# Hybrid decoder trunk on one core: from the output projection to layer 1's projection, each stage's last part also prepares the next stage's first weights and tiles, and x is stored tile by tile

## The chip, the core and the metric

The kernel runs on one core of a Trainium2 chip. Its engines run side by side, each with its own queue of instructions: TensorE (PE, matrix products and transposes; PEld is its weight load), VectorE (DVE), ScalarE (ACT), GpSimd (POOL) and SyncE (SP), which issues the transfers (DMA) between the chip's memory and the on-chip buffers. They wait for each other only through semaphores. The metric is the time of one execution on the device in microseconds (us); lower is better.

## What is computed

Two decoder layers on x (1024 tokens x 1024 features, float32). Layer 0 mixes with two attentions of 8 heads each (one with a forget bias, one on 256 keys picked by an indexer), layer 1 with 16 heads of dilated attention. What follows the attention is the same in both layers, and it is what the change touches, with layer 1's first projection:

```python
x = x + merged @ w_out[i]                               # output projection
h = rmsnorm(x, norm_ffn[i])
x = x + conv_ffn(h, w_gate[i], w_up[i], conv_w[i], conv_b[i], w_down[i])
gate = jax.nn.sigmoid(rmsnorm(x, norm_ple[i]) @ w_ple_gate[i])
x = x + gate * (p[i] @ w_ple_proj[i])
...
def conv_ffn(h, w_gate, w_up, conv_w, conv_b, w_down):
    g = causal_dwconv(h @ w_gate, conv_w, conv_b)       # width 3, along the tokens
    return (jax.nn.gelu(g) * (h @ w_up)) @ w_down       # 2816 hidden features
```

`rmsnorm(x, g)` is x times the reciprocal root of its mean square over the features, times g.

## The kernel before

x stays on chip as 8 tiles of 128 tokens. The trunk (`trunk`) is a row of stages. From the attention of layer 0 on they are: output projection (`l0out`, function `output_stage`), feed-forward (`l0ff`, `ffn_stage`), per-layer gate (`l0pg`, `ple_stage`), layer 1's projection (`l1in`, `projection_stage`), layer 1's attention (`l1dil`), `l1out`, `l1ff`, `l1pg`, and a last stage, `load_stage`, that writes all of x with one transfer. Between two stages stands `recycle`: semaphores are cleared and all engines meet at a barrier, so that nothing of a stage begins before everything of the one ahead has ended. A stage's buffers are taken when it begins and given back when it ends.

**Products in three passes.** Every operand is split into a rounded part (hi) and the rest (lo), and `mm3` (L68 to L70) issues hi x lo, lo x hi and hi x hi: three matmuls of 128x128 by 512 columns. Weights arrive in a `raw` buffer with two places in chunks of 512 KB; ScalarE rounds a chunk to hi (128x1024) and GpSimd takes the rest, lo (128x1024; in the feed-forward's loop VectorE does that). The next chunk of a place is loaded once the lo of the old one is done.

**Feeding the tiles.** The class `Feed` turns x's tiles into the stationary or moving operands of a stage. For tile t: `square` (ScalarE, L129: sum of squares), `root` (GpSimd, L138 and L140: reciprocal root), `scale` (VectorE, L148: x times root times gain into one of two `xn` buffers), `turn` (TensorE, L160: 8 transposes of 128x128 into two banks of PSUM), `round` (ScalarE, L170: hi, twice 128x512) and `rest` (VectorE, L176: lo, twice 128x512). `ready` lets TensorE wait for the rest of a tile. In `output_stage` the tiles of `merged` need no norm, so there only turn, round and rest run.

**The stages.** `output_stage` and `projection_stage` walk over strips of 512 output columns (2 and 6), and in each over the 8 tiles; one unit (strip, tile) is 24 matmuls. Feed's first two tiles are turned before unit 0, and tile t + 2 after unit t of the first strip. The unit's sum is added to x (or copied) from one of four banks (`acc`). `ple_stage` has 16 units of 30 matmuls (24 for the gate, 6 for p's product), tiles 0 to 3 with strip 0, with strip 1, then tiles 4 to 7. `ffn_stage` runs 11 groups; a group is 4 units of 48 matmuls (two blocks of 128 hidden features, two halves of the tokens, gate and up), then 16 down products of 6 matmuls (m = 0 to 15, two for each tile), which use four banks in turn; VectorE adds each to x (L1952). Group 0 is written out and the other ten are a loop; ahead of group 0 tiles 0 to 3 are turned, tiles 4 to 7 in the middle of its first unit, and unit 1 waits until tile 7 is ready.

What sets the order is the program text of each engine; there is no planner. The last instructions of a stage are products and additions only, and the first ones of the next load the gain and the first weights, round them and feed the first tiles.

## Time and profile before

| | us |
|---|---|
| median of 3 runs (lowest to highest) | 3448.13 (3444.61 to 3450.27) |
| the profiled execution | 3450.76 |
| its span, first to last instruction | 3449.0 |
| TensorE busy | 3213.1 (93%) |
| VectorE / ScalarE / GpSimd busy | 1850.1 / 1269.2 / 729.8 |
| mean granted TensorE clock | 0.968 of full |

The profile has a page of totals, and the trace can be asked for waits, for the instructions of a stretch in order of time, for the busy time of stretches and for transfers. A row of the order in time gives the start, the length, the engine, the line, what is written from what, how many alike follow each other (x8), and in square brackets how long the engine had been idle before it and what it waited for. A start plus a length is an end. The length of a matmul overlaps the next, so the distance from start to start is its cost. Names carry the stage: `l0ff_d` is a tile of the feed-forward of layer 0, `k_x` is x.

### The profile page before, as it was taken

To read this page: it belongs to the slowest core of one execution; us is meant where nothing else is said; L and a number is where in the kernel's file an instruction comes from. 1 tells how busy PE (TensorE), PEld (TensorE's weight loads), DVE (VectorE), ACT (ScalarE), POOL (GpSimd) and SP (SyncE) were. 2 spreads that over 40 slices of the span, in tenths; PEclk is the share of its full clock that TensorE was granted. 3 is DMA by queue.
4 is the path that set the end of the run, shared out by engine and by line. 5 is a ranking of instruction groups with operands and counts; after the bars stand their busy time and mean duration, and the time that the engine had idled before them with its cause. 6 is when DMAs were issued, how large, how long until landed. Compare 5 with 4: busy or idle time off the path is not lost. (4 is left out here: it accounts for less than half of the span.)

```text
span 3449.0 us, 44902 instructions
## 1 busy us (share of the span) xinstructions
PE 3213.1 (93%) x15622; PEld 2673.8 (78%) x15622; DVE 1850.1 (54%) x3192; ACT 1269.2 (37%) x2716; POOL 729.8 (21%) x443
## 2 busy tenths in 40 slices
PE   7889997979979999999998998899879999999988
PEld 6657886968768888888776886799768888888866
DVE  4599997878234444444443331899324444443442
ACT  3274525868132222222132211788323222222231
POOL 3005444253220000000031541775220000000030
PEclk9999998989989999999999999899989999999999
DMA  4202233131221111111021323322112111111021
GB/s 138 73 21 92 92 116 81 37 69 37 97 68 61 55 42 49 45 52 36 5 74 52 95 97 122 70 67 54 49 31 86 49 44 53 49 37 61 0 79 49
DMA packets 268632, 214.55 MB, mean 62 GB/s; under 512 B 95164, under 2 KB 220908, under 8 KB 268524
## 3 DMA queue, kind: packets, MB, share of 16 engines
q1 hardware_dynamic: 268524, 213.17, 20.7%
q8 instruction: 60, 0.98, 0.1%
q14 instruction: 48, 0.39, 0.0%
HBM read 170.67 MB, written 41.94 MB: 62 GB/s over the span
## 5 line engine op out<-in xcount | busy, mean ns | idle before, releaser
L1961 DVE SCALAR_TENSOR_TENSOR l1ff_c<-l1ff_g,l1ff_cw,l1ff_c 128x512 f32<-128x512 f32 x44 | 33.1, 752 | 251.3 <-ACT l1ff_c L1870 251.3
L1961 DVE SCALAR_TENSOR_TENSOR l0ff_c<-l0ff_g,l0ff_cw,l0ff_c 128x512 f32<-128x512 f32 x44 | 33.1, 752 | 251.3 <-ACT l0ff_c L1870 251.3
L1750 DVE TENSOR_SCALAR_CACHE_REDUCE k_x<-k_x,l0in_cand 128x384 bf16<-128x384 f32 (+1 forms) x186 | 163.7, 942 | 1.1
L1952 DVE TENSOR_TENSOR k_x<-l0ff_d,k_x 128x512 f32<-128x512 f32 x176 | 119.4, 689 | 80.8 <-PE l0ff_d L70 80.8
L1952 DVE TENSOR_TENSOR k_x<-l1ff_d,k_x 128x512 f32<-128x512 f32 x176 | 119.4, 689 | 80.8 <-PE l1ff_d L70 80.8
L68 PE MATMUL l1in_acc<-l1in_w_lo,l1h_hi 128*128 128x512 f32 x384 | 151.1, 393 | 4.4 <-POOL l1in_w_lo L508 4.3
L69 PE MATMUL l1in_acc<-l1in_w_hi,l1h_lo 128*128 128x512 f32 x384 | 150.0, 391 | 0.0
L70 PE MATMUL l1in_acc<-l1in_w_hi,l1h_hi 128*128 128x512 f32 x384 | 149.9, 390 | 0.0
L132 POOL MEMSET l0pg_mhalf<- 128x8 f32 x1 | 0.1, 105 | 687.1 <-POOLq L107 687.1
L132 POOL MEMSET l1pg_mhalf<- 128x8 f32 x1 | 0.1, 104 | 687.1 <-POOLq L107 687.1
L68 PE MATMUL l1ff_gu<-l1ffn_lo,l1ff_w_hi_g 128*128 128x512 f32 x352 | 138.4, 393 | 7.4 <-DVE l1ff_cw L2000 5.5
L68 PE MATMUL l0ff_gu<-l0ffn_lo,l0ff_w_hi_g 128*128 128x512 f32 x352 | 137.8, 392 | 7.4 <-DVE l0ff_cw L2000 5.5
L70 PE MATMUL l1ff_gu<-l1ffn_hi,l1ff_w_hi_g 128*128 128x512 f32 x352 | 138.0, 392 | 0.0
L69 PE MATMUL l1ff_gu<-l1ffn_hi,l1ff_w_lo_g 128*128 128x512 f32 x352 | 138.0, 392 | 0.0
L70 PE MATMUL l0ff_gu<-l0ffn_hi,l0ff_w_hi_g 128*128 128x512 f32 x352 | 137.6, 391 | 0.0
L69 PE MATMUL l0ff_gu<-l0ffn_hi,l0ff_w_lo_g 128*128 128x512 f32 x352 | 137.5, 391 | 0.0
L68 PE MATMUL l0ff_gu<-l0ffn_lo,l0ff_w_hi_u 128*128 128x512 f32 x352 | 137.1, 390 | 0.0
L68 PE MATMUL l1ff_gu<-l1ffn_lo,l1ff_w_hi_u 128*128 128x512 f32 x352 | 137.1, 390 | 0.0
L70 PE MATMUL l1ff_gu<-l1ffn_hi,l1ff_w_hi_u 128*128 128x512 f32 x352 | 137.1, 389 | 0.0
L69 PE MATMUL l1ff_gu<-l1ffn_hi,l1ff_w_lo_u 128*128 128x512 f32 x352 | 137.1, 389 | 0.0
L70 PE MATMUL l0ff_gu<-l0ffn_hi,l0ff_w_hi_u 128*128 128x512 f32 x352 | 137.1, 389 | 0.0
L69 PE MATMUL l1ff_d<-l1ff_w_hi_d,l1ff_a_lo 128*128 128x512 f32 x352 | 137.1, 389 | 0.0
(465 smaller groups left out, 9720.6 us busy)
## 6 DMA issues: line engine op xcount, KB each, us to landing
l0w_raw<-in_w_in_even SPq DMA_DIRECT2D x24, 512.0 KB, 4.1
l1in_raw<-in_w_in_odd SPq DMA_DIRECT2D x24, 512.0 KB, 3.8
l0ff_raw_g<-in_w_gate SPq DMA_DIRECT2D x22, 512.0 KB, 4.0
l0ff_raw_u<-in_w_up SPq DMA_DIRECT2D x22, 512.0 KB, 5.3
l0ff_raw_d<-in_w_down SPq DMA_DIRECT2D x22, 512.0 KB, 4.9
l1ff_raw_g<-in_w_gate SPq DMA_DIRECT2D x22, 512.0 KB, 4.0
l1ff_raw_u<-in_w_up SPq DMA_DIRECT2D x22, 512.0 KB, 5.2
l1ff_raw_d<-in_w_down SPq DMA_DIRECT2D x22, 512.0 KB, 4.9
```

The costliest lines, as they stand in the source:

```text
L68: pe.matmul(out, a_hi, b_lo, start=start, stop=False)
L69: pe.matmul(out, a_lo, b_hi, start=False, stop=False)
L70: return pe.matmul(out, a_hi, b_hi, start=False, stop=stop)
L132: pool.memset(self.half[:], -0.5).then_inc(self.mean, 1)
L1750: tick(dve.tensor_scalar(hits[:, cols], score[:, cols], cand[:, i:i + 1].bitcast(F32), 0.0, ALU.is_ge, ALU.add, accum_out=cnt[:, i:i + 1]))
L1952: dve.tensor_tensor(cols, ps_d[:, m % 4, :], cols, ALU.add).then_inc(added, 1)
L1961: dve.scalar_tensor_tensor(c[:, half, :], g[:, at - 1:at + 511], cw[:, 1, bass.ds(blk, 1)], c[:, half, :], ALU.mult, ALU.add).then_inc(con ...
```

## The change

**Two feeds in a stage.** Where a stage has a successor, its last part runs the successor's steps besides its own, with a second feed (`nfeed`) and a second set of semaphores (`n_...`):

- `output_stage`: once all of merged is turned, SP loads the norm gain and the feed-forward's first two blocks of gate and up weights; when strip 0 is done (8 units) ScalarE rounds them (4 pieces of 128x1024), GpSimd takes the 4 rests and only then the roots; tiles 0 to 6 of x are squared, scaled, turned, rounded and rested during strip 1, tile t being turned after unit t + 1 of the strip. Tile 7 (`LAST`) is left to the feed-forward, which turns it in the middle of its first unit, with the convolution's weights.
- `ffn_stage`: the last of the 11 groups is written out for TensorE too. SP loads the gate stage's gain, its first five weight chunks and half of p once the last group's weights are split; ScalarE rounds the chunks after its last unit, with squares of tiles 0 to 4 between them; GpSimd alternates rests and roots; VectorE scales and rests tiles 0 and 1 between the additions of the last down products; TensorE turns them after tile 4 and tile 5 of the down products.
- `ple_stage` of layer 0: four squares and two tiles of `l1in` are fed during units 8 to 11, its first strip of weights is split during units 12 to 15.
- The stages that follow begin with that done: a few `sem_inc` stand for it, and their feeds begin at tile `first` (2, or 7 in the feed-forward), their roots at `first_root`.

**Fixed places.** So that a stage's operands outlive its barrier, the buffers of these stages lie at fixed addresses (`sb(..., at=)`): hi and lo of the tiles, the strips, and a region for the rest, shared one after the other. Two tiles of `l1in` go to slots that the gate stage no longer reads (`slot`).

**The store.** `load_stage` and the barrier ahead of it are gone; in layer 1's gate stage SP writes tile t of x (512 KB) once its last addition is done.

The shapes of the loads, roundings, transposes and matmuls, and what each stage multiplies, stay as they are. Of the stages ahead of `l0out` and of `l1dil` nothing moves. The diff, cut to the moved steps:

```diff
...
+MERGED_AT, HI_AT, LO_AT, STRIP_AT = (32 * n * KB for n in range(4))
+EXTRA_AT, SMALL_AT = 160 * KB, 172 * KB
...
     def scale(self, dve, t):
+        n = t - self.first
         if t == 0:
             dve.wait_ge(self.gain_in, 16)
-        if t >= 2:
-            dve.wait_ge(self.turned, 2 * (t - 1))
-        dve.wait_ge(self.rooted, t + 1)
-        dve.scalar_tensor_tensor(self.xn[:, t % 2, :], self.src[:, t, :], self.rstd[:, t:t + 1], self.g[:],
+        if n >= 2:
+            dve.wait_ge(self.turned, 2 * (n - 1))
+        if t >= self.first_root:
+            dve.wait_ge(self.rooted, t - self.first_root + 1)
...
+        feed = Feed(st, x, hi, lo, [[tp[:, 2 * i + h, :] for h in range(2)] for i in range(2)], ident, buf.gain, buf.norm,
+                    slot=buf.slot, first=AHEAD, first_root=ROOTS)
...
+            for b in range(2):
+                sp.sem_inc(raw_in[b], 16 * CH // 2)
...
+            act.sem_inc(hi_ready, CH)
...
-            feed.scale(dve, 0)
-            feed.scale(dve, 1)
-            feed.rest(dve, 0)
-            feed.scale(dve, 2)
-            feed.rest(dve, 1)
+            feed.scale(dve, AHEAD)
...
-            feed.turn(pe, 0)
-            feed.turn(pe, 1)
...
+            sp.wait_ge(feed.turned, 2 * NT)
+            nfeed.load(sp)
+            for b in range(2):
+                for dst, src in zip(nxt.raw, nxt.sources):
+                    sp.dma_start(dst[:, b, :].rearrange("p (k n) -> p k n", n=P),
+                                 src[:, b * P:(b + 1) * P].rearrange("(k p) n -> p k n", p=P)).then_inc(n_raw_in[b], 16)
...
+            act.wait_ge(filled, NT)
+            split_next(0)
+            split_next(1)
+            for t in range(AHEAD):
+                act.wait_ge(added, NT + t + 1)
+                nfeed.square(act, t)
+                if t:
+                    nfeed.round(act, t - 1)
+            nfeed.round(act, AHEAD - 1)
...
+            nfeed.prepare(pool)
+            for k in range(4):
+                n, b = k % 2, k // 2
+                pool.wait_ge(n_hi_ready, k + 1)
+                pool.tensor_tensor(nxt.w_lo[n][:, b, :], nxt.raw[n][:, b, :], nxt.w_hi[n][:, b, :].bitcast(F32),
+                                   ALU.subtract).then_inc(n_lo_ready, 1)
+            for t in range(AHEAD):
+                nfeed.root(pool, t)
...
+                if s == 1 and t:
+                    nfeed.rest(dve, t - 1)
+                if s == 1 and t < AHEAD:
+                    nfeed.scale(dve, t)
...
+                if s == 1 and t:
+                    nfeed.turn(pe, t - 1)
...
+            if nxt is not None:
+                sp.wait_ge(lo_ready, CH)
+                nxt.load(sp, 0, n_raw_in[0])
+                nxt.load(sp, 1, n_raw_in[1])
+                sp.wait_ge(feed.scaled, NT - AHEAD)
+                nfeed.load(sp)
+                for n in range(2, nxt.CH):
+                    sp.wait_ge(n_lo_ready, n - 1)
+                    nxt.load(sp, n, n_raw_in[n % 2])
+            else:
+                for t in range(NT):
+                    sp.wait_ge(added, t + 5 if t < 4 else t + 9)
+                    sp.dma_start(final[t * P:(t + 1) * P, :], x[:, t, :]).then_inc(stored, 16)
+                sp.wait_ge(stored, 16 * NT)
...
+                if i < CH - 2:
+                    split(2 + i)
+                if nxt is not None and i >= 12:
+                    n = i - 12
+                    act.wait_ge(n_raw_in[n % 2], 16 * (n // 2 + 1))
+                    act.activation(nxt.chunk(0, n)[0], nxt.raw[:, n % 2, :, :], ACT.Copy).then_inc(n_hi_ready, 1)
+                if nxt is not None and 8 <= i < 8 + nxt.ROOTS:
+                    act.wait_ge(added, i - 3)
+                    nfeed.square(act, i - 8)
+                if nxt is not None and 10 <= i < 10 + nxt.AHEAD:
+                    nfeed.round(act, i - 10)
...
+                if nxt is not None and i == 9:
+                    dve.wait_ge(feed.turned, 2 * (NT - AHEAD))
+                if nxt is not None and 9 <= i < 9 + nxt.AHEAD:
+                    nfeed.scale(dve, i - 9)
+                if nxt is not None and 10 <= i < 10 + nxt.AHEAD:
+                    nfeed.rest(dve, i - 10)
...
-            feed.turn(pe, 0)
...
-            feed.turn(pe, 1)
...
+                if nxt is not None and 9 <= i < 9 + nxt.AHEAD:
+                    feed.ready(pe, i - 3)
+                    nfeed.turn(pe, i - 9)
...
+            for n in range(2):
+                for b in range(2):
+                    sp.sem_inc(raw_in[n][b], 16)
...
+            sp.wait_ge(w_lo_done, 6 * NG)
+            nfeed.load(sp)
+            for n in range(nxt.CH):
+                if n >= 2:
+                    sp.wait_ge(n_lo_ready, n - 1)
+                nxt.load(sp, n, n_raw_in[n % 2])
+            nxt.load_p(sp, 0, n_p_in)
+            sp.wait_ge(n_p_in, 16)
...
+            act.sem_inc(w_hi_done, 4)
+            feed.square(act, LAST)
+            feed.round(act, LAST)
...
+            def square_next(t):
+                act.wait_ge(added, 16 * NG - 10 + 2 * t)
+                nfeed.square(act, t)
+
+            for n in range(nxt.CH):
+                if n == nxt.CH - 1:
+                    act.wait_ge(lo_done, 4 * NG)
+                act.wait_ge(n_raw_in[n % 2], 16 * (n // 2 + 1))
+                act.activation(nxt.chunk(0, n)[0], nxt.raw[:, n % 2, :, :], ACT.Copy).then_inc(n_hi_ready, 1)
+                if n >= 2:
+                    square_next(n - 2)
+            nfeed.round(act, 0)
+            square_next(3)
+            nfeed.round(act, 1)
+            square_next(4)
...
+            pool.sem_inc(w_lo_done, 4)
...
+            nfeed.prepare(pool)
+            for n in range(nxt.CH):
+                pool.wait_ge(n_hi_ready, n + 1)
+                n_hi, n_lo = nxt.chunk(0, n)
+                pool.tensor_tensor(n_lo, nxt.raw[:, n % 2, :, :], n_hi.bitcast(F32), ALU.subtract).then_inc(n_lo_ready, 1)
+                if n >= 2:
+                    nfeed.root(pool, n - 2)
+            for t in range(nxt.CH - 2, nxt.ROOTS):
+                nfeed.root(pool, t)
...
+                    if last and m % 2 == 1 and m >= 7:
+                        t = (m - 7) // 2
+                        if t < nxt.AHEAD:
+                            nfeed.scale(dve, t)
+                        if 1 <= t < 1 + nxt.AHEAD:
+                            nfeed.rest(dve, t - 1)
...
+                        if feeding and b == 0 and half == 1:
+                            feed.ready(pe, LAST)
...
+                            if feeding and b == 0 and half == 0 and n == 0:
+                                pe.wait_ge(cw_in, 32)
+                                pe.transpose(ps_gu[:, 1, 1, 0:4 * NFB], cw4[:], ident[0:4 * NFB, 0:4 * NFB]).then_inc(cw_t, 1)
+                                feed.turn(pe, LAST)
...
+                    if last and 4 <= t < 4 + nxt.AHEAD:
+                        nfeed.turn(pe, t - 4)
...
-            with pe.Fori(0, NG - 1) as i:
...
+            with pe.Fori(0, NG - 2) as i:
...
+            body(NG - 1, True)
...
-        load_stage(nc, "store", [(tiles(out[0]), x[:])])
...
```

VectorE, from the last additions of `l0out` (`l0out_acc`) into the feed-forward; `l0ff_raw_d` serves as the feed-forward's `xn`, `l0ffn_lo` and `k_lo` are the tiles' rests. Before:

```order
L652 TENSOR_TENSOR k_x<-l0out_acc,k_x 128x512 x11
L87 UNCONDITIONAL_BRANCH
L1939 UNCONDITIONAL_BRANCH
L1989 MEMSET l0ff_g 128x2
L148 SCALAR_TENSOR_TENSOR l0ff_raw_d<-k_x,l0ff_rstd,l0ff_gain 128x1024 x2
L176 TENSOR_TENSOR l0ffn_lo<-l0ff_d,l0ffn_hi 128x4x128 x2
```

The same place now:

```order
L757 TENSOR_TENSOR k_x<-l0out_acc,k_x 128x512 x4
L164 SCALAR_TENSOR_TENSOR l0ff_raw_d<-k_x,l0ff_rstd,l0ff_gain 128x1024
L757 TENSOR_TENSOR k_x<-l0out_acc,k_x 128x512
L193 TENSOR_TENSOR k_lo<-l0out_tp,k_hi 128x4x128 x2
L164 SCALAR_TENSOR_TENSOR l0ff_raw_d<-k_x,l0ff_rstd,l0ff_gain 128x1024
```

The first scale stands between the additions of units 8 and 9, and from then on each addition is followed by the rests of one tile and the scale of the next; the branches (the stage's end) come seven tiles later.

VectorE at the end of `l0ff`, in the last group's down products. Before:

```order
L1973 TENSOR_TENSOR l0ff_a_lo<-l0ff_act_f,l0ff_a_hi 128x512
L1952 TENSOR_TENSOR k_x<-l0ff_d,k_x 128x512 x14
L87 UNCONDITIONAL_BRANCH
L793 UNCONDITIONAL_BRANCH
L148 SCALAR_TENSOR_TENSOR l0pg_xn<-k_x,l0pg_rstd,l0pg_gain 128x1024 x2
```

The same place now:

```order
L2094 TENSOR_TENSOR l0ff_a_lo<-l0ff_act_f,l0ff_a_hi 128x512
L2073 TENSOR_TENSOR k_x<-l0ff_d,k_x 128x512 x6
L164 SCALAR_TENSOR_TENSOR l0pg_xn<-k_x,l0pg_rstd,l0pg_gain 128x1024
L2073 TENSOR_TENSOR k_x<-l0ff_d,k_x 128x512 x2
L164 SCALAR_TENSOR_TENSOR l0pg_xn<-k_x,l0pg_rstd,l0pg_gain 128x1024
L193 TENSOR_TENSOR k_lo<-l0ff_gu,k_hi 128x4x128 x2
L2073 TENSOR_TENSOR k_x<-l0ff_d,k_x 128x512 x2
L193 TENSOR_TENSOR k_lo<-l0ff_gu,k_hi 128x4x128 x2
L2073 TENSOR_TENSOR k_x<-l0ff_d,k_x 128x512 x4
```

The first scale now stands ahead of the additions m = 8 to 15, the second scale and the rests of two tiles ahead of the later ones.

## Rows read from the trace of the kernel before

**Rows 1.** The page, part 1: busy us, share of the span, instructions.

```profile
PE 3213.1 (93%) x15622; PEld 2673.8 (78%) x15622; DVE 1850.1 (54%) x3192; ACT 1269.2 (37%) x2716; POOL 729.8 (21%) x443
```

**Rows 2.** Order in time, l0out to l0ff: start, length, engine, line, tiles, [idle].

```profile
968.63 0.69 DVE L652 TENSOR_TENSOR k_x<-l0out_acc,k_x 128x512 f32<-128x512 f32 x1 [4.75 <-PE l0out_acc L70]
970.14 0.33 SPq L124 DMA_DIRECT2D l0ff_gain<-in_norm_ffn  x1
975.79 3.67 PE L160 MATMUL l0ff_d<-k_square,l0ff_raw_d 128*128 128x128 f32 x16 [7.21 <-DVE l0ff_raw_d L148]
1012.59 0.47 PE L68 MATMUL l0ff_gu<-l0ffn_lo,l0ff_w_hi_g 128*128 128x512 f32 x1 [1.94 <-issue]
```

**Rows 3.** Order in time, l1out to l1ff: TensorE's first row and unit 1.

```profile
2550.06 3.67 PE L160 MATMUL l1ff_d<-k_square,l1ff_raw_d 128*128 128x128 f32 x16 [7.26 <-DVE l1ff_raw_d L148]
2588.16 0.47 PE L68 MATMUL l1ff_gu<-l1ffn_lo,l1ff_w_hi_g 128*128 128x512 f32 x1 [1.94 <-issue]
```

**Rows 4.** Order in time, l0out: units with turns, then an addition without.

```profile
894.07 1.04 PE L160 MATMUL l0out_tp<-k_square,l0m_merged 128*128 128x128 f32 x8
900.44 1.03 PE L160 MATMUL l0out_tp<-k_square,l0m_merged 128*128 128x128 f32 x8
925.18 0.69 DVE L652 TENSOR_TENSOR k_x<-l0out_acc,k_x 128x512 f32<-128x512 f32 x1 [4.75 <-PE l0out_acc L70]
```

**Rows 5.** Order in time: one step each of square, root, scale, lo and hi.

```profile
972.52 1.06 ACT L129 ACTIVATE l0ff_g<-k_x 128x1024 f32<-128x1024 f32 x1
974.03 0.55 POOL L140 TENSOR_TENSOR l0ff_rstd<-l0ff_ss,l0ff_mhalf 128x1 f32<-128x1 f32 x1
979.03 1.28 DVE L148 SCALAR_TENSOR_TENSOR l0ff_raw_d<-k_x,l0ff_rstd,l0ff_gain 128x1024 f32<-128x1024 f32 x1
896.83 2.40 POOL L638 TENSOR_TENSOR l0out_w_lo<-l0out_raw,l0out_w_hi 128x1024 fp32r<-128x1024 f32 x1 [18.25 <-ACT l0out_w_hi L621]
1727.54 1.06 ACT L733 ACTIVATE l0pg_w_hi<-l0pg_raw 128x1024 fp32r<-128x1024 f32 x1 [3.53 <-DMA l0pg_raw<-in_w_ple_gate]
```

**Rows 6.** Order in time, last group of l0ff to l0pg's unit 1.

```profile
1698.11 0.39 PE L68 MATMUL l0ff_d<-l0ff_w_lo_d,l0ff_a_hi 128*128 128x512 f32 x1
1702.66 0.63 ACT L1877 ACTIVATE l0ff_a_hi<-l0ff_act_f 128x512 fp32r<-128x512 f32 x1 [0.84 <-DVE l0ff_act_f L1969]
1720.07 0.69 DVE L1952 TENSOR_TENSOR k_x<-l0ff_d,k_x 128x512 f32<-128x512 f32 x1 [0.67 <-PE l0ff_d L70]
1748.93 0.48 PE L68 MATMUL l0pg_ps_g<-l0pg_w_lo,l0pg_hi 128*128 128x512 f32 x1
```

**Rows 7.** Order in time, the same of layer 1: last addition, turn ahead of unit 1.

```profile
3295.68 0.69 DVE L1952 TENSOR_TENSOR k_x<-l1ff_d,k_x 128x512 f32<-128x512 f32 x1 [0.67 <-PE l1ff_d L70]
3325.24 1.10 PE L160 MATMUL l1pg_tp<-k_square,l1pg_xn 128*128 128x128 f32 x8
```

**Rows 8.** Order in time, l0pg to l1in: last addition, first turn of the dense part.

```profile
1858.08 0.69 DVE L821 TENSOR_TENSOR k_x<-k_x,l0pg_sg 128x512 f32<-128x512 f32 x1
1880.52 1.04 PE L160 MATMUL l1in_tp<-k_square,l1in_xn 128*128 128x128 f32 x8
```

**Rows 9.** Last addition; transfers: count, KB each, median us to landing.

```profile
3435.34 0.69 DVE L821 TENSOR_TENSOR k_x<-k_x,l1pg_sg 128x512 f32<-128x512 f32 x1
...
vsplit<-l1in_vout SPq DMA_DIRECT2D x16, 512.0 KB, 2.6
...
l0pg_raw<-in_w_ple_gate SPq DMA_DIRECT2D x8, 512.0 KB, 3.8
```

**Rows 10.** Stretch, length, busy PE PEld DVE ACT POOL, granted clock, DMA share, GB/s.

```profile
864.00:868.00 4.00, 0.04 (x1) 0.00 (x0) 1.23 (x2) 2.60 (x3) 2.31 (x2) 0.93 0.58 219
867.00:871.00 4.00, 2.82 (x7) 2.27 (x8) 0.00 (x0) 0.00 (x0) 3.37 (x2) 0.60 0.41 119
1873.00:1877.00 4.00, 0.84 (x4) 0.67 (x4) 1.88 (x3) 3.25 (x5) 2.74 (x2) 1.00 0.33 115
```

More of the change, by code:

```diff
@@ L203, in index_projection_stage @@
         tp = st.ps("tp", [P, 4, 512])
-        feed = Feed(st, x, hi, lo, [[tp[:, 2 * i + h, :] for h in range(2)] for i in range(2)], ident, gain, junk=feat[:])
+        norm = Norm(st, st.sb("xn", [P, 2, D]), feat[:], st.sb("gain", [P, D]))
+        feed = Feed(st, x, hi, lo, [[tp[:, 2 * i + h, :] for h in range(2)] for i in range(2)], ident, gain, norm)
         square_in, tail_in, angle_in = st.sem("square_in"), st.sem("tail_in"), st.sem("angle_in")
@@ L403, in _, with __init__, slot, chunk @@
                         mm.then_inc(tok_done, 1)
-def projection_stage(nc, name, x, gain, hi, lo, ident, strips, proj, vsplit, stats):
-    S = len(strips)
+class HeadsBuffers:
+    CH = 4
+    AHEAD = 2
+    ROOTS = 4
+    def __init__(self, st, hi, lo, gain, strips):
+        self.hi, self.lo, self.gain, self.strips = hi, lo, gain, strips
+        self.raw = st.sb("raw", [P, 2, KD // self.CH, 512], at=MERGED_AT)
+        self.w_hi = [st.sb(f"w_hi{b}", [P, KD, 512], F32R, at=STRIP_AT + 32 * b * KB) for b in range(2)]
+        self.w_lo = [st.sb(f"w_lo{b}", [P, KD, 512], F32R, at=STRIP_AT + (32 * b + 16) * KB) for b in range(2)]
+        self.norm = Norm(st, st.sb("xn", [P, 2, D], at=MERGED_AT + 8 * KB), st.sb("junk", [P, D], at=MERGED_AT + 16 * KB)[:],
+                         st.sb("gain", [P, D], at=MERGED_AT + 24 * KB), SMALL_AT + 256)
+    def slot(self, t):
+        return (t + self.AHEAD) % NT
+    def chunk(self, s, c):
+        rows = (slice(None), slice(c * KD // self.CH, (c + 1) * KD // self.CH))
+        return self.w_hi[s % 2][rows], self.w_lo[s % 2][rows]
+    def load(self, sp, n, arrived):
+        s, c = n // self.CH, n % self.CH
+        size = D // self.CH
+        sp.dma_start(self.raw[:, n % 2, :, :], self.strips[s][c * size:(c + 1) * size, :]
+                     .rearrange("(k p) n -> p k n", p=P)).then_inc(arrived, 16)
@@ L421, in projection_stage @@
         acc = st.ps("acc", [P, 4, 512])
         tp = st.ps("tp", [P, 4, 512])
-        feed = Feed(st, x, hi, lo, [[tp[:, 2 * i + h, :] for h in range(2)] for i in range(2)], ident, gain)
+        feed = Feed(st, x, hi, lo, [[tp[:, 2 * i + h, :] for h in range(2)] for i in range(2)], ident, buf.gain, buf.norm,
+                    slot=buf.slot, first=AHEAD, first_root=ROOTS)
         raw_in = [st.sem(f"raw_in{b}") for b in range(2)]
@@ L517, in _ @@
             pool.memset(half[:], -0.5).then_inc(rstd_step, 1)
+            pool.sem_inc(lo_ready, CH)
             feed.prepare(pool)
-            feed.root(pool, 0)
-            feed.root(pool, 1)
-            low(0)
-            low(1)
-            feed.root(pool, 2)
-            low(2)
-            low(3)
-            for t in range(3, NT):
+            for t in range(ROOTS, NT):
                 feed.root(pool, t)
@@ L718, in _ @@
-            feed.load(sp)
-            load(0)
-            load(1)
-            load_p(0)
-            for n in range(2, 2 * CH):
-                load(n)
-                if n == CH:
-                    sp.wait_ge(p_turned, 2)
-                    load_p(1)
+            for n in range(CH, 2 * CH):
+                if n >= CH + 2:
+                    sp.wait_ge(lo_ready, n - CH - 1)
+                buf.load(sp, n, raw_in[n % 2])
+            sp.wait_ge(p_turned, 2)
+            buf.load_p(sp, 1, p_arrived)
@@ L742, in _ @@
-            feed.square(act, 1)
-            split(0)
-            feed.round(act, 0)
-            split(1)
-            feed.square(act, 2)
             p_round(0)
             p_round(1)
-            split(2)
-            feed.round(act, 1)
-            split(3)
-            split(4)
-            for t in range(3, NT):
+            for t in range(ROOTS, NT):
                 feed.square(act, t)
+            split(0)
+            split(1)
             for i, (s, t) in enumerate(UNITS):
@@ L807, in _ @@
             p_rest(1)
-            feed.rest(dve, 1)
             feed.scale(dve, 3)
```

446 lines of the change are left out of this document (206 added, 240 removed).

## The prediction

> **What bounds the kernel now.** I read the page's totals first: TensorE is busy 3213.1 of 3449.0 us [rows 1], so only its idle time can be won without taking work away. Then I asked for its instructions in order of time around each end of a stage; the reader is to see there how long it idles and what it waits for. The places are alike. The last product of l0out ends at 975.79 - 7.21 = 968.58, the last addition at 969.32; SyncE issues the next stage's first load at 970.14, so the barrier costs 0.8 us. Then everything hangs on the gain's load, the scales and the first weights, and TensorE is dense and undisturbed only from unit 1 on, at 1012.59 [rows 2]. There are five such ends: two out to feed-forward, two feed-forward to gate, one gate to layer 1's projection; a sixth is the store. Inside the stages TensorE is the bound: without turns an addition waits 4.75 us and takes 0.69, a pitch of 5.44 for 24 matmuls (0.227 each); with a turn it is 900.44 - 894.07 = 6.37 [rows 4]. So a turn moved into dense work costs 0.92 us, and 30 matmuls cost 6.80.
>
> I cost each end as an interval: from the last product of a stage to a point in the next from which both kernels do the same.
>
> **Out to feed-forward.** Before: 1012.59 - 968.58 = 44.0 us in layer 0 [rows 2], 2588.16 - (2550.06 - 7.26) = 45.4 in layer 1 [rows 3]. Now, counted from the same product:
> - Seven turns during strip 1: 7 x 0.92 = 6.4.
> - A wait ahead of the first of them. The four roundings start when strip 0 is done, about 925.2 [rows 4]; GpSimd needs four rests, each 2.40 [rows 5], from 926.3 to 936.0, and only then takes the first root (0.55 and a small step before it, 0.8), so VectorE's scale (1.28) ends at 938.2, while TensorE wants tile 0 at 936.0: 2.3 us. VectorE's addition behind it slips too, but four banks cover it. From the second tile on the loop addition, square (1.06 and the read of its sum, 1.25), root 0.8, scale 1.28, with two rests of 0.69 between, takes about 5.3 of the 6.37 us between two turns: 1 us of slack, no further wait.
> - The tail: after the last turn, round and rest, which the row at 1012.59 prices at 1.94 (there too TensorE waits for the last tile's rest), and the barrier 0.8: 2.8.
> - The feed-forward's unit 0, 48 matmuls = 10.9 with one turn and the small transpose of the convolution's weights, 1.0. The tile's square, root and scale (3.4) end before the first half (5.4); the convolution's two small loads now stand first in SyncE's queue.
>
> Sum 6.4 + 2.3 + 2.8 + 11.9 = 23.4. **Gain 20.6 and 22.0.** The loads (2.6 MB from about 914 on, when SyncE has nothing left) have 11 us until ScalarE wants them; they lie beside products.
>
> **Feed-forward to gate.** Let D be the start of the last group's down products, 1698.11; before, the last addition ends at 1720.76 = D + 22.7, and unit 1 of the gate stage starts at 1748.93 = D + 50.8 [rows 6]. In layer 1 the last addition ends at 3296.37, and unit 1 follows the turn at 3325.24 by 0.9: 29.7 us later against 28.2 [rows 7]. Now the chain of the first tile decides. ScalarE's last unit ends at 1703.3 = D + 5.2 [rows 6]; then chunk 0 is rounded (1.06 [rows 5]) to D + 6.3, its rest (2.4) to 8.9, chunk 2's load, which waits for that place, to 12.7 (3.8 to landing [rows 9]), rounding 13.8, rest 16.2, and only then root(0) 17.0, scale 18.4. TensorE has come to the first turn at D + 13.6 (10 products of 1.36): it waits 4.8 us. The rest follows from the same durations: load 4 to D + 20.1, its rounding and a square to 22.4, round(0) 23.5, rest(0) 24.3, the additions m = 10 and 11, rest(1) 26.8, last product 28.4, last addition D + 29.4, that is 6.7 later than before. In the gate stage: barrier 0.8, p's eight transposes 0.9, unit 0 6.8, a turn 0.9: unit 1 at D + 38.8 against D + 50.8. **Gain 12.0 and 13.6.** Here the edit gives a new wait, and queued behind the waiting scale are the additions m = 8 to 15, for which TensorE's four banks wait.
>
> **Gate to layer 1's projection.** Two turns during units 9 and 10 cost 1.8. The squares, the two scales and the weight chunks (one per unit of 6.8; load, rounding, rest together 7.3, in two places) lie beside products. The last addition ends at 1858.77; the next stage's unit 0 begins after 0.8 at 1859.6 + 1.8 = 1861.4, and ends at 1866.8, where it meets the turn that stood at 1880.52 [rows 8]. **Gain 13.7.**
>
> **Store.** Before, 3449.0 - 3436.0 = 13.0 us stand after the last addition [rows 9]. Now only the last tile's 512 KB are outstanding: the other direction (chip memory to buffer) of that size takes 3.8 to landing, the kernel's own writes of that size 2.6 [rows 9]; I take the writes, being the same kind, and 0.6 around them: 3.3. Bounds 3.2 to 5. **Gain 9.7.**
>
> **The clock.** After TensorE has idled, its granted clock may fall from 2.4 to 1.2 GHz. In the stretch 864 to 868 it was busy 0.04 us, and in 867 to 871 the clock was 0.60; yet in 1873 to 1877, with 3.2 us idle, it stayed at 1.00 [rows 10]. The new version has seven waits of 2.3 to 4.8 us: two at the first turn, two of 2.8 and one of about 3 at barriers, two of 4.8. A stretch like 867 to 871 (0.4 of 4 us lost) costs 1.6; I let three of the seven meet it: 5 us lost, bounds 0 and 11. The Trainium skill (TensorE: Matmul & The Clock Gate, Part 1) says that a gap drops the clock to half, that when it happens depends on where the gap falls, and advises against idle gaps between bursts of matmuls: that speaks against the new waits. [...]
>
> **Sum.** 20.6 + 22.0 + 12.0 + 13.6 + 13.7 + 9.7 = 91.6, less 5 = 86.6. The profiled execution took 3450.76, 1.8 above its span and 2.6 above the median; 3448.1 - 86.6 = 3361.5, so **3362 us**. What isn't in the sum: everything ahead of l0out, l1in's later strips and l1dil have the same instructions in the same order, cost 0. ScalarE's order has as many table loads as before (8), so squares between gelu and sigmoid add none. TensorE's last group written out instead of looped: no price in the trace, but straight text runs at the loop's pitch; taken as 0, bounds 0 to 3 for two.
>
> **Rivals.**
> - *The chain of the tiles is slower than its slack.* In strip 1 square, root, rest and scale have 1 us of slack per tile, and GpSimd and VectorE share the work. If every turn waited 1.5 us more, 2 x 7 x 1.5 = 21, and if the last group's waits grew by 2 us each, 4: 3387. For it: five steps over three engines, each passed on by a semaphore. Against it: every duration has a row, and the handovers are small beside them. Chance 0.17, at 3372 to 3390.
> - *The waits I reckon are not there.* If GpSimd's rests are quicker beside an idle VectorE or the chunk loads land sooner, 4 x 2 us come back, and no clock falls: 5 more: 3349. Chance 0.13, at 3345 to 3354.
> - *The next stage doesn't start at once.* The preparation is done, but the first product still waits, for its stage's code or for a semaphore. Then each of five ends would keep some 7 us of the idle time: 3397. The row at 970.14 shows an engine active 0.8 us after the last addition, which speaks against it. Chance 0.04.
> - *Slower than before: the fixed places.* All operands of TensorE move to new addresses. If a matmul there cost more, the two feed-forwards alone have 6336 of them (44 units x 48 and 176 x 6, twice): from 0.014 us each, 6% of 0.227, on, the gain of 87 is eaten. With 10% it would be 3362 + 144 = 3506. Against it: the pitch of 0.227 is that of l0out and of the down products (1.36 for 6) alike, whose buffers lie apart. Chance 0.02.
>
> **How the numbers follow.** The forecast, 3354 to 3372, has 0.64; its size hangs on the clock (0 to 11) and the two waits. Two in ten may lie outside: the range takes in all of the forecast, nearly all of the second rival and the nearer part of the first, 3349 to 3384. A measurement of this kernel tells 0.2% (7 us) from no change; only the last rival is on the other side. Faster 0.97, within 0.2% 0.01, slower 0.02.
>
> **What would show it.** Right: TensorE's wait ahead of the first turn in strip 1 is 2 to 3 us and absent ahead of the other six; the idle time between l0out and l0ff is 3 us instead of 26 with turns; in the last group TensorE waits some 5 us for a scale behind `root`, and the stage ends 6 to 7 us later after D; l1in's first product comes 3 us after the last of l0pg; 3 to 4 us between the last addition and the end. Wrong: a wait at each turn (first rival), a first product that waits for "issue" (third), a pitch above 5.44 for a unit (fourth), or a clock at half in more than three of the seven places.

## The result, and the profile after

The changed kernel takes 3372.4 us (median of 4 runs, 3370.4 to 3373.2) against 3448.8 for the kernel before (again 4 runs); the ratio is 0.978, 95% interval 0.976 to 0.980. It is faster by 76 us, 10 less than the forecast of 86.6: inside the range of 3349 to 3384, and 0.4 above the upper end of the forecast's own 3354 to 3372. Measured again later in another series it took 3372.2 (3368.1 to 3375.8).

The page of the changed kernel, totals, to be held against [rows 1]:

```profile
PE 3198.6 (95%) x15622; PEld 2663.5 (79%) x15622; DVE 1850.8 (55%) x3192; ACT 1268.2 (38%) x2716; POOL 729.2 (22%) x448
```

The work is the same; the span is 3371.1, so TensorE's idle time fell from 235.9 to 172.5 us. The remaining 14.5 of the 77.9 us of span are busy time: fewer matmuls run at half clock (the mean granted clock is 0.977 where it was 0.968).

**Out to feed-forward.** The changed kernel in order of time; these rows answer to [rows 2, 3]:

```profile
932.94 1.96 PE L177 MATMUL l0out_tp<-k_square,l0ff_raw_d 128*128 128x128 f32 x8 [2.22 <-DVE l0ff_raw_d L164]
940.98 1.04 PE L177 MATMUL l0out_tp<-k_square,l0ff_raw_d 128*128 128x128 f32 x8
...
976.85 0.47 PE L73 MATMUL l0ff_gu<-k_lo,l0ff_w_hi_g 128*128 128x512 f32 x1 [3.06 <-PEq L2168]
984.07 1.04 PE L177 MATMUL l0ff_d<-k_square,l0ff_raw_d 128*128 128x128 f32 x8
...
2515.44 0.47 PE L73 MATMUL l1ff_gu<-k_lo,l1ff_w_hi_g 128*128 128x512 f32 x1 [3.08 <-PEq L2168]
```

The first turn waits 2.22 us, the other six not at all, and the feed-forward's first product comes 3.06 us behind the last one of the stage ahead (3.08 in layer 1). So the stalls are where they were reckoned. What is longer is busy time: from the first turn to the second 8.04 us instead of 6.37, from the first product of the feed-forward to the turn of tile 7 7.22 instead of 5.44.

**Feed-forward to gate.** The last group, VectorE, GpSimd and TensorE together (the last row is p's transposes, the gate stage's first work on TensorE); they answer to [rows 6]:

```profile
1675.86 0.39 PE L73 MATMUL l0ff_d<-l0ff_w_lo_d,l0ff_a_hi 128*128 128x512 f32 x1
...
1692.68 2.34 POOL L2054 TENSOR_TENSOR l0pg_x_lo<-l0pg_raw,l0pg_x_hi 128x1024 fp32r<-128x1024 f32 x1
1692.81 3.28 DVE L164 SCALAR_TENSOR_TENSOR l0pg_xn<-k_x,l0pg_rstd,l0pg_gain 128x1024 f32<-128x1024 f32 x1 [5.18 <-POOL l0pg_rstd L154]
...
1696.15 1.97 PE L177 MATMUL l0ff_gu<-k_square,l0pg_xn 128*128 128x128 f32 x8 [6.53 <-DVE l0pg_xn L164]
1696.74 2.37 POOL L2054 TENSOR_TENSOR l0pg_p_lo<-l0pg_raw,l0pg_p_hi 128x1024 fp32r<-128x1024 f32 x1
1697.22 2.98 DVE L164 SCALAR_TENSOR_TENSOR l0pg_xn<-k_x,l0pg_rstd,l0pg_gain 128x1024 f32<-128x1024 f32 x1
...
3235.14 1.97 PE L177 MATMUL l1ff_gu<-k_square,l1pg_xn 128*128 128x128 f32 x8 [6.92 <-DVE l1pg_xn L164]
...
3249.54 1.06 PE L934 MATMUL l1pg_ps_p<-k_square,l1pg_ptile 128*128 128x128 f32 x8 [1.73 <-PEq L115]
```

The scale is an instruction of 1.28 us [rows 5]. Here it takes 3.28 and 2.98, both times beside a rest that GpSimd began just before it. TensorE waits 6.53 us in layer 0 and 6.92 in layer 1 where 4.8 was reckoned; unit 1 of the gate stage starts at D + 43.0 in layer 0 and D + 43.6 in layer 1, not at 38.8.

**Gate to projection, and the end.** Rows that answer to [rows 8, 9]:

```profile
1831.82 0.47 PE L73 MATMUL l1in_acc<-k_w_lo,k_hi 128*128 128x512 f32 x1 [3.02 <-PEq L115]
1837.39 1.04 PE L177 MATMUL l1in_tp<-k_square,k_xn 128*128 128x128 f32 x8
...
3367.34 0.69 DVE L923 TENSOR_TENSOR k_x<-k_x,l1pg_sg 128x512 f32<-128x512 f32 x1
3368.06 0.33 SPq L832 DMA_DIRECT2D out<-k_x  x1
```

The first product of layer 1 comes 3.02 us after the last of the gate stage; 3.0 us stand between the last addition and the end, where 13.0 stood before.

**The clock.** The 6 us that follow each of the seven idle stretches of the changed kernel (columns as in [rows 10]; the granted clock is the third number from the end):

```profile
932.94:938.94 6.00, 6.00 (x24) 5.16 (x25) 3.03 (x4) 2.12 (x4) 0.75 (x2) 0.72 0.01 3
976.85:982.85 6.00, 6.00 (x19) 4.79 (x20) 1.28 (x1) 0.59 (x2) 0.74 (x2) 0.72 0.03 8
1696.15:1702.15 6.00, 6.00 (x21) 5.07 (x22) 5.84 (x6) 3.59 (x7) 5.22 (x6) 0.60 0.01 3
1831.82:1837.82 6.00, 6.00 (x28) 4.97 (x29) 1.28 (x1) 0.23 (x1) 0.18 (x2) 1.00 0.31 90
2473.19:2479.19 6.00, 6.00 (x31) 5.12 (x32) 3.03 (x4) 2.12 (x4) 0.76 (x2) 1.00 0.01 3
2515.44:2521.44 6.00, 6.00 (x19) 4.78 (x20) 1.28 (x1) 0.60 (x2) 0.74 (x2) 0.72 0.03 9
3235.14:3241.14 6.00, 6.00 (x20) 5.10 (x21) 6.00 (x6) 3.81 (x7) 5.26 (x6) 0.56 0.06 22
```

TensorE's clock has two levels, 1.2 and 2.4 GHz, so 0.72 over 6 us means that part of them ran at 1.2 GHz; 0.28 x 6 = 1.7 us of work are lost. That is the 1.67 and nearly all of the 1.8 by which the stretches above are longer. The clock fell behind five of the seven: 0.28, 0.28, 0.40, 0.28 and 0.44 of 6 us, 10.1 us in all.

### The profile page after: what moved, and what is told of

Same layout as the page of the kernel before. It is cut to its first block and busy times, and to the rows that moved or that the text cites. A ratio compares the mean times of both kernels' runs of the same rounds, so it can differ in the third digit from the quotient of the medians.

```text
span 3371.1 us, 44871 instructions
## 1 busy us (share of the span) xinstructions
PE 3198.6 (95%) x15622; PEld 2663.5 (79%) x15622; DVE 1850.8 (55%) x3192; ACT 1268.2 (38%) x2716; POOL 729.2 (22%) x448
## 5 line engine op out<-in xcount | busy, mean ns | idle before, releaser
L73 PE MATMUL l1in_acc<-k_w_lo,k_hi 128*128 128x512 f32 x384 | 150.2, 391 | 3.1 <-PEq L115 3.0
L75 PE MATMUL l1in_acc<-k_w_hi,k_hi 128*128 128x512 f32 x384 | 149.5, 389 | 0.0
L74 PE MATMUL l1in_acc<-k_w_hi,k_lo 128*128 128x512 f32 x384 | 149.4, 389 | 0.0
L73 PE MATMUL l1ff_gu<-k_lo,l1ff_w_hi_g 128*128 128x512 f32 x352 | 137.7, 391 | 3.1 <-PEq L2168 3.1
L73 PE MATMUL l0ff_gu<-k_lo,l0ff_w_hi_g 128*128 128x512 f32 x352 | 137.7, 391 | 3.1 <-PEq L2168 3.1
L73 PE MATMUL l1ff_d<-l1ff_w_lo_d,l1ff_a_hi 128*128 128x512 f32 x352 | 137.9, 392 | 0.0
L73 PE MATMUL l0ff_d<-l0ff_w_lo_d,l0ff_a_hi 128*128 128x512 f32 x352 | 137.9, 392 | 0.0
L75 PE MATMUL l0ff_gu<-k_hi,l0ff_w_hi_g 128*128 128x512 f32 x352 | 137.6, 391 | 0.0
L75 PE MATMUL l1ff_gu<-k_hi,l1ff_w_hi_g 128*128 128x512 f32 x352 | 137.6, 391 | 0.0
L74 PE MATMUL l1ff_gu<-k_hi,l1ff_w_lo_g 128*128 128x512 f32 x352 | 137.5, 391 | 0.0
```

The costliest lines, as they stand in the source:

```text
L73: pe.matmul(out, a_hi, b_lo, start=start, stop=False)
L74: pe.matmul(out, a_lo, b_hi, start=False, stop=False)
L75: return pe.matmul(out, a_hi, b_hi, start=False, stop=stop)
```

## The experiments

All start from the changed kernel. Theory A says what cost the ff-to-gate ends their gain: a scale that meets GpSimd's rest stands until the rest is done. Theory C says what cost the out-to-ff ends theirs: half clock behind idle stretches.

### E1: the rests wait for the scale

```diff
             for n in range(nxt.CH):
                 pool.wait_ge(n_hi_ready, n + 1)
+                if n >= 3:
+                    pool.wait_ge(nfeed.scaled, n - 2)
                 n_hi, n_lo = nxt.chunk(0, n)
```

> The changed kernel; in the last feed-forward group GpSimd takes the rests of weight chunks 3 and 4 only once VectorE's scale of tile 0, or tile 1, is done. Theory A (a scale, which reads two operands from the on-chip buffer, stands still while GpSimd takes a rest): both scales (L164) of l0ff and l1ff fall from 3.28 and 2.98 us to about 1.28, TensorE's wait ahead of the first turn from 6.5 to 4.6, and the stage ends some 2 us sooner after the start of the down products, though GpSimd's rests are 1.4 us later. Rival B (the scales are long for another reason, such as ScalarE's work or TensorE's transposes at the half clock): they stay near 3 us, the wait stays 6.5, and the stage ends no sooner, or 1 us later.

Layer 0's last group in this kernel, VectorE, GpSimd, TensorE:

```profile
1696.30 1.28 DVE L164 SCALAR_TENSOR_TENSOR l0pg_xn<-k_x,l0pg_rstd,l0pg_gain 128x1024 f32<-128x1024 f32 x1 [5.37 <-POOL l0pg_rstd L154]
1697.64 1.97 PE L177 MATMUL l0ff_gu<-k_square,l0pg_xn 128*128 128x128 f32 x8 [4.72 <-DVE l0pg_xn L164]
1697.72 2.35 POOL L2056 TENSOR_TENSOR l0pg_x_lo<-l0pg_raw,l0pg_x_hi 128x1024 fp32r<-128x1024 f32 x1 [1.53 <-DVE l0pg_xn L164]
```

All four scales are back at 1.28 or 1.29 us, and TensorE waits 4.72 and 4.65, as the prediction had reckoned with 1.28. Unit 1 of the gate stage starts at D + 40.5 in both layers, 2.5 and 3.1 earlier than in the changed kernel. Of that the shorter wait is 1.8 and 2.3; the rest, 0.7 to 0.8, is clock, which in the 6 us behind the wait is 0.74 and 0.72 here and was 0.60 and 0.56. The 1.7 that remain to 38.8 are what 0.74 and 0.72 still cost. The single run, 3370.3, is 2 us below the changed kernel, which one run can't tell from its scatter; the verdict rests on the rows. (The rows gain 5.6 us; but in this execution the clock also fell behind layer 1's first turn in the output stage and ahead of layer 1's projection, 1.7 us each, where the changed kernel's kept it.)

### E2a and E2b: the same collision made, and avoided, in the output stage

There the changed kernel takes all four rests, then the roots, and no scale meets a rest. E2a takes root 0 behind the second rest, so that the third meets the scale; E2b also holds the third rest until the scale is done (the line with the wait; E2a lacks it).

```diff
             for k in range(4):
                 n, b = k % 2, k // 2
+                if k == 2:
+                    nfeed.root(pool, 0)
+                    pool.wait_ge(nfeed.scaled, 1)
                 pool.wait_ge(n_hi_ready, k + 1)
...
-            for t in range(AHEAD):
+            for t in range(1, AHEAD):
                 nfeed.root(pool, t)
```

> The changed kernel; in the output stage GpSimd takes the root of tile 0 after two of the four weight rests instead of after all four, and the third rest follows at once, beside VectorE's scale of tile 0. If the 2.2 us wait ahead of the first turn came from the root's place alone, it is gone (the root is ready 3 us sooner, and the scale takes 1.28). Theory A (a scale stands still beside a rest) says that the first scale now takes 2.4 + 1.3 = about 3.5 us, and that some 1 us of the wait stays in both layers.

> As the run before, but the third weight rest waits until tile 0's scale is done. Theory A: the scale takes 1.28 us, no wait ahead of the first turn (2.2 us before), output stages 2.2 us shorter each, and 1 to 2 us more where the wait had let TensorE's clock fall. Rival B: the same as the run before, whatever its scale took.

E2a in layer 0, then E2b in the same place:

```profile
930.53 2.39 POOL L742 TENSOR_TENSOR l0ff_w_lo_g<-l0ff_raw_g,l0ff_w_hi_g 128x1024 fp32r<-128x1024 f32 x1
930.68 3.31 DVE L164 SCALAR_TENSOR_TENSOR l0ff_raw_d<-k_x,l0ff_rstd,l0ff_gain 128x1024 f32<-128x1024 f32 x1 [2.23 <-POOL l0ff_rstd L154]
934.05 1.09 PE L177 MATMUL l0out_tp<-k_square,l0ff_raw_d 128*128 128x128 f32 x8 [0.89 <-DVE l0ff_raw_d L164]
```

```profile
930.88 1.28 DVE L164 SCALAR_TENSOR_TENSOR l0ff_raw_d<-k_x,l0ff_rstd,l0ff_gain 128x1024 f32<-128x1024 f32 x1 [2.23 <-POOL l0ff_rstd L154]
932.24 2.40 POOL L743 TENSOR_TENSOR l0ff_w_lo_g<-l0ff_raw_g,l0ff_w_hi_g 128x1024 fp32r<-128x1024 f32 x1 [1.48 <-DVE l0ff_raw_d L164]
933.20 1.03 PE L177 MATMUL l0out_tp<-k_square,l0ff_raw_d 128*128 128x128 f32 x8
```

The collision can be made at will: 3.31 us where the changed kernel has 1.28, and gone again with the one wait. The idle stretch of 2.2 at the first turn was GpSimd's order, rests first: 0.89 with the collision, none without, in both layers. One run each, 3365.6 and 3364.5, so 7 and 8 us below the changed kernel and too close to tell them apart; what tells them apart is the rows.

### E3: squares ahead of the third chunk, each root behind its rest

```diff
-            for n in range(nxt.CH):
+            def split_next(n):
...
-                if n >= 2:
-                    square_next(n - 2)
+            split_next(0)
+            split_next(1)
+            for t in range(3):
+                square_next(t)
+            split_next(2)
             nfeed.round(act, 0)
+            split_next(3)
             square_next(3)
             nfeed.round(act, 1)
+            split_next(4)
             square_next(4)
...
-                if n >= 2:
-                    nfeed.root(pool, n - 2)
-            for t in range(nxt.CH - 2, nxt.ROOTS):
-                nfeed.root(pool, t)
+                nfeed.root(pool, n)
```

> The changed kernel; in the last feed-forward group ScalarE squares tiles 0 to 2 before it rounds chunk 2, and GpSimd takes root n right after the rest of chunk n (not of chunk n + 2). By the chain of the prediction with theory A: root(0) is ready near D + 9.3 (D: start of the last down products), so no wait ahead of the first turn, and the last addition falls at about D + 24.3 instead of D + 33.3: 9 us less for each of two layers, 18 in all, near 3354. Rival: the end of the stage hangs on the last weight chunk's load, rounding and rest and not on the tiles; then it ends at D + 28 or later and the gain is under 10 us in all.

3356.5 us (3356.0 to 3357.4; ratio to the kernel before 0.973, 0.971 to 0.975), 16 below the changed kernel. In layer 0:

```profile
1691.01 1.37 DVE L164 SCALAR_TENSOR_TENSOR l0pg_xn<-k_x,l0pg_rstd,l0pg_gain 128x1024 f32<-128x1024 f32 x1
1692.93 1.03 PE L177 MATMUL l0ff_gu<-k_square,l0pg_xn 128*128 128x128 f32 x8
1693.73 2.81 DVE L164 SCALAR_TENSOR_TENSOR l0pg_xn<-k_x,l0pg_rstd,l0pg_gain 128x1024 f32<-128x1024 f32 x1
1696.60 1.09 PE L177 MATMUL l0ff_gu<-k_square,l0pg_xn 128*128 128x128 f32 x8
```

No turn waits. The first tile was late because its root stood behind the third chunk, whose load waits for a place in `raw`; the tile itself was done long before. Unit 1 is at D + 34.2 and D + 34.3, so 8.8 and 9.3 earlier than in the changed kernel: 18.1 in the rows, 16 in the medians. The second scale still meets a rest (2.81), and here that costs nothing, since TensorE has two down products (2.7 us) to do meanwhile.

### E4: TensorE busy up to the barrier

Six matmuls more behind the last turn of the output stage, into a bank that nobody reads:

```diff
                 if s == 1 and t:
                     nfeed.turn(pe, t - 1)
+            pe.wait_ge(added, NT * S - 1)
+            for k in range(6):
+                pe.matmul(acc[:, 0, :], hi[:, k, 7 * P:8 * P], w_hi[1][:, k, :], start=k == 0, stop=k == 5)
```

> Starts from the changed kernel. After the last prepared turn of the output stage TensorE runs six matmuls more, whose result nobody reads (a hi tile and weights that lie there), so that it stands idle only across the barrier. Theory C (about 1.7 us of the shortfall of each output stage's end is TensorE at half clock in the first matmuls of the feedforward, after the two idle stretches of 2.2 and 3.1 us in front of them): the stretch idle ahead of the feedforward falls from 3.07 to about 1.8, its first half unit takes 5.4 instead of 7.2 us in both layers, and the span is 3 to 4 us shorter (3367.5). Rival D (the clock falls because of the stretch of 2.2 us before the first turn, or with the place in the program whatever stands before it): the first half unit stays at 7.2 and the span within 1 us of the changed kernel's 3371.

Layer 0:

```profile
974.73 1.63 PE L785 MATMUL l0out_acc<-l0out_w_hi,k_hi 128*128 128x512 f32 x6
978.07 0.47 PE L73 MATMUL l0ff_gu<-k_lo,l0ff_w_hi_g 128*128 128x512 f32 x1 [1.71 <-PEq L2171]
983.71 1.04 PE L177 MATMUL l0ff_d<-k_square,l0ff_raw_d 128*128 128x128 f32 x8
```

The idle stretch is 1.71 us (1.69 in layer 1), and the first half unit takes 5.64 and 5.63 us instead of 7.22 and 7.23, as theory C expects. By itself this trace doesn't show it, since C9 below has the same 5.63 without the six matmuls. Over the eleven traces of kernels with the change the clock fell behind 14 of the 18 stretches of 3.1 us at this place, and behind none of the four of 1.7 (here and in E8); that supports theory C. Rival D is out: the stretch of 2.2 us at the first turn is still there in this kernel, and in E2a, E2b and E7, where it is gone, the clock fell at this place behind five of six. The median, 3369.1 (3366.3 to 3370.5), is 3.3 lower; the expected 3 to 4 are no more than what two runs of one kernel differ by, as C9 shows.

### C9: the changed kernel once more

> The changed kernel as it is, in the same series as the kernel above, so that the two are compared on one chip: 3372 us, its scales beside GpSimd's rests again near 3.1 us each in the feedforward's last group, and waits of 2.2 and 6.7 us at the first turns. Rival (these were chance of one execution): scales at 1.28 and waits of 4.8.

```profile
979.93 0.47 PE L73 MATMUL l0ff_gu<-k_lo,l0ff_w_hi_g 128*128 128x512 f32 x1 [3.06 <-PEq L2168]
985.56 1.04 PE L177 MATMUL l0ff_d<-k_square,l0ff_raw_d 128*128 128x128 f32 x8
...
1694.77 3.29 DVE L164 SCALAR_TENSOR_TENSOR l0pg_xn<-k_x,l0pg_rstd,l0pg_gain 128x1024 f32<-128x1024 f32 x1 [5.64 <-POOL l0pg_rstd L154]
```

The scales are long again (3.29 and 3.17, 3.28 and 2.98), the waits 2.22, 2.21, 6.99 and 6.84: theory A is no accident of one execution. But the half unit behind 3.06 us of idle time takes 5.63 here: the same kernel with the same idle stretch kept its clock this time, and this execution, the fastest of its five, has a span of 3366.4, 4.7 shorter. So what an idle stretch costs in clock differs from execution to execution, and E4's gain by its median can't be told from that.

### E5: the store as before

```diff
-            else:
+            elif final is not None:
...
-                ple_stage(nc, L + "pg", x, ple, ident, final=out[0])
+                ple_stage(nc, L + "pg", x, ple, ident)
+                recycle(nc)
+        with Stage(nc, "store") as st:
...
+                sp.dma_start(out[0].rearrange("(t p) c -> p t c", p=P), x[:]).then_inc(moved, 16)
+                sp.wait_ge(moved, 16)
```

> Undoes the store alone: in layer 1's gate stage the last additions write x again and the whole of x goes out behind the stage in one transfer of 4 MB, as in the kernel before. The theory (the store by tiles gives 9.7 to 9.9 us, all of it at the end): 3382 us, the time from the last addition to the end of the span back at 15.1 from 5.1 us. Rival (part of that gain was lost again ahead of the end, because fifteen transfers that leave during the stage slow its weights or the additions): under 9, the stage's last products earlier than in the changed kernel by the difference.

```profile
3366.03 0.69 DVE L923 TENSOR_TENSOR k_x<-k_x,l1pg_sg 128x512 f32<-128x512 f32 x1
3367.54 0.38 SPq L2259 DMA_DIRECT2D out<-k_x  x1
```

3384.1 us (3381.4 to 3385.8), 11.7 above the changed kernel. From the last addition to the end of the span (3379.6) it is 12.9 against 3.0: 9.9 for the store. (The 15.1 and 5.1 of the expectation count from the last product; measured 15.0 and 5.1.) Ahead of the end there is no sign of a price: from unit 1 of layer 1's gate stage to its last product it is 107.7 us here and 107.5 in the changed kernel, with the transfers beside it. The medians differ by 1.8 more than the rows, which is within the scatter of the runs.

### E6: no tiles ahead for layer 1's projection

`HeadsBuffers` with `AHEAD = 0` and `ROOTS = 0`: the weights are still prepared in the gate stage, the two tiles are squared, scaled, split and turned in the projection's own.

> Undoes one part of the last boundary alone: layer 0's gate stage still prepares the weights of layer 1's projection, but not its first two tiles; these are squared, scaled, split and turned in the projection's own stage. The theory (at this boundary the turned tiles are worth more than the weights, whose halves come early in the stage anyhow): the first product unit of layer 1's projection starts about 8.7 us later behind the last product than in the changed kernel, less the 1.8 us that the two turns no longer take in the gate stage: 3379.3 us. Rival (the weights carry the gain, and the tiles' chain hides behind their arrival): within 2 us of 3372.

```profile
1837.27 3.78 PE L177 MATMUL l1in_tp<-k_square,k_xn 128*128 128x128 f32 x16 [6.67 <-DVE k_xn L164]
...
1846.36 1.03 PE L177 MATMUL l1in_tp<-k_square,k_xn 128*128 128x128 f32 x8
```

3376.7 us (3373.4 to 3379.7), 4.4 above the changed kernel; 6.9 was expected and at most 2 by the rival. From the end of l0pg's last product to the turn of tile 2 it was 1880.52 - 1856.7 = 23.8 us before, is 1846.36 - 1830.6 = 15.8 here and 1837.39 - 1828.8 = 8.6 in the changed kernel. So the weights alone bring 8.0 to 8.1, the tiles 7.2 less the 1.8 of their two turns, 5.3 to 5.4, together the 13.4 of this end. That the tiles are worth more than the weights was wrong.

### E7: both repairs; E8: with the six matmuls too

E7 is E3 and E2b in one, E8 adds E4's edit.

> Both repairs together, on the changed kernel: at the feedforward's end ScalarE squares tiles 0 to 2 before it copies chunk 2, and GpSimd takes each root right behind the rest of the same number; at the output stage's end GpSimd takes the first root before its third weight rest, and holds that rest until the first scale is done. The theory has the two gains add, since they lie at different ends: 16 us from the first, 6 to 8 from the second (two ends, 2.2 us of wait and up to 1.8 us of clock each): 3349 us, no wait at any first turn. Rival (the second's gain is no more than the two waits of 2.2 us, since the clock falls at the barrier anyhow): 3352. A second rival: the clock's mean falls as the stage ends close up, and it stays at 3355.

> The two repairs together with the six matmuls that keep TensorE busy to the output stage's barrier. In the kernel with the two repairs the first half unit of the feedforward took 7.24 us in layer 0 and 7.21 in layer 1, behind idle stretches of 3.06 and 3.11. Theory C, that this is TensorE at half clock and costs 1.6 us at each end: both fall to 5.6, the idle stretches to 1.7, and the time to 3345. Rival: the half clock then comes at another stretch idle (the boundary of 3.0 us ahead of layer 1's projection), and the time stays at 3348.

E7: 3348.4 us (3346.5 to 3352.0), ratio 0.971 (0.969 to 0.972). E8: 3345.0 (3343.0 to 3347.8), ratio 0.970 (0.968 to 0.971). No first turn waits in either; the gains of the two ends add: 24 us below the changed kernel. In E8 the half units behind the barrier take 5.64 and 5.63 us, in E7 7.24 and 7.21. But in E8 the clock was low elsewhere. These are the 6 us behind the idle stretch of 3.02 us ahead of layer 1's projection:

```profile
1818.69:1824.69 6.00, 6.00 (x14) 4.75 (x15) 1.28 (x1) 0.00 (x0) 0.18 (x2) 0.50 0.33 90
```

Half clock throughout, 3 us lost, as the rival had it for this place. The two intervals overlap, so whether E8 is faster than E7 isn't settled; that both beat the changed kernel is.

## Why the prediction was right, and where it was short

The waits came at the places where they were reckoned, and released by what was said; but one step of the chain left out that VectorE and GpSimd hold each other up, and the clock was charged too low. By the changed kernel's trace:

| term | reckoned | measured |
|---|---|---|
| out to ff, layer 0 / layer 1 | 20.6 / 22.0 | 17.0 / 20.0 |
| ff to gate, layer 0 / layer 1 | 12.0 / 13.6 | 7.8 / 8.8 |
| gate to projection | 13.7 | 13.4 |
| store | 9.7 | 9.9 |
| clock | -5 | in the terms above, -10.1 |
| elsewhere | 0 | +1.0 |
| sum | 86.6 | 77.9 |

- **Out to ff: right.** The wait was reckoned at 2.3 and is 2.22, the other six turns wait for nothing (so the slack of 1 us per tile was there), the tail 2.8 and is 3.06. What is missing is mostly clock: 1.7 and 1.6 in layer 0 and 1.6 in layer 1 (7.22 against the 5.63 that the same half unit takes at full clock).
- **Ff to gate: the step that failed.** It is "root(0) 17.0, scale 18.4": the scale at its own length of 1.28, with GpSimd's next rest at its side. E1 gives that step back and lands on the reckoned wait, 4.72 for 4.8. The longer waits cost 1.7 and 2.1 us; the rest of the 9.0 missing in the two terms is nearly all clock behind them, 2.4 and 2.6. By E1 the step cost 2.5 + 3.1 = 5.6 us with the clock that goes with it, the larger part of the 8.7 by which the span's gain fell short of the forecast. The trace of before had shown it. Behind the row from which the price was taken [rows 5], at 979.03, stands the rest that met it, and in the gate stage an addition of two operands from the on-chip buffers (a `TENSOR_TENSOR` of 0.69 alone) meets another:

```profile
979.42 3.12 POOL L1927 TENSOR_TENSOR l0ff_w_lo_g<-l0ff_raw_g,l0ff_w_hi_g 128x1024 fp32r<-128x1024 f32 x1 [4.84 <-ACT l0ff_w_hi_g L1854]
...
1754.11 2.39 POOL L777 TENSOR_TENSOR l0pg_w_lo<-l0pg_raw,l0pg_w_hi 128x1024 fp32r<-128x1024 f32 x1
1754.43 2.62 DVE L821 TENSOR_TENSOR k_x<-k_x,l0pg_sg 128x512 f32<-128x512 f32 x1
...
1781.13 0.69 DVE L821 TENSOR_TENSOR k_x<-k_x,l0pg_sg 128x512 f32<-128x512 f32 x1
```

 Whoever comes second pays. At 979 the scale was first, and the rest took 3.12 instead of 2.40; at 1754 the rest was first, and the addition took 2.62. The price of 1.28 was read where the other engine had paid.
- **Gate to projection and store: right**, within 0.3.
- **The clock: right in kind, small in size.** Three of seven stretches at 1.6 were charged; in this execution it was five at 1.7 to 2.6, 10.1 us. That is chance as much as error: in C9's execution of the same kernel it was three of the seven, 5.6 us. The advice of the Trainium skill (TensorE: Matmul & The Clock Gate, Part 1) against idle gaps between bursts of matmuls was borne out at five of the seven here and at three there.
- **The rivals.** Half of the first one came true: the waits of the last group grew by 1.7 and 2.1 us where it said 2 each, and the reason lies in its own words, that GpSimd and VectorE share the work. Its other half, a wait at each turn, did not, and that half carried 21 of its 25 us; the result at the lower end of its range owes as much to the clock. The second rival had no waits at all, and they came. No product waits for its stage to start (the idle stretches at barriers are 1.7 to 3.1 us, which are last addition and barrier), and a unit without a turn still has a pitch of 5.44 in the output stage and in layer 1's projection, so no cost of the new addresses shows.

## What to carry to other kernels

Preparing the next stage under the products of this one pays as reckoned, if each step is priced beside the neighbour that it will have, not by its length where it stood alone or came first. Where a stage's end still waits, look for what stands in the queue ahead of the small instruction that everything hangs on: here a reciprocal root of 0.55 us stood behind rests of 2.4 in one stage and behind a load in another, and moving it was worth 24 us (E7), a third of what the whole change had brought. The stretches of 2.2 us and longer in which TensorE stood idle cost some 1.7 us of clock behind them most of the times, and up to 2.6 behind the longest; a sum is to carry that for each. How many are hit differs from execution to execution: 10.1 us in one of the changed kernel, 5.6 in another.
